# A two-layer attention and mixture-of-experts decoder: where the expert weights are kept first, and the router's stretch by quarters

## What is computed

```
h  = x + W_out( sum_b sigmoid(g_b(xn)) * (branch_b(xn) @ W_branch_b) ),  xn = RMSNorm(x)   # the mixer, three branches
xn = RMSNorm(h)
group  = top-1 of 4 (softmax of xn @ w_rg + b_rg)
expert = top-2 of the 8 in that group (xn @ w_re + b_re), weights renormalised, times the group's
out = h + sum over the chosen experts of w * ( silu(xn @ w1[e]) * (xn @ w3[e]) ) @ w2[e]     # 32 experts, 256 hidden
```

## Time and profile before

| | |
|---|---|
| three runs, median (range) | 1061.05 us (1058.94 to 1063.56) |
| the profiled execution: its own time, its span | 1065.5 us, 1063.8 us |
| TensorE matmul, weight load, VectorE, ScalarE, share of the span | 90%, 73%, 45%, 44% |
| granted TensorE clock, mean | 0.968 |
| HBM read | 291 MB, mean 275 GB/s |
| layer 0: mixer, router, experts | to 290 us, to 322 us, to 529 us |
| layer 1: mixer, router, experts | from 538 us to 815 us, to 847 us, to 1056 us |

### The profile page before, as it was taken

One profiled execution on the slowest core, in us unless ns is written; L12 is line 12 of the kernel. 1 busy time (PEld: TensorE's weight loads), 2 busy tenths in 40 slices (PEclk: granted clock), 3 DMA queues, 4 the chain that ended last, 5 costly groups with the idle time before them and its releaser, 6 DMA issues. The chain is left out here.

```text
span 1063.8 us, 19005 instructions
## 1 busy us (share of the span) xinstructions
PE 960.0 (90%) x7790; PEld 774.5 (73%) x7790; DVE 481.7 (45%) x805; ACT 472.1 (44%) x714; POOL 21.6 (2%) x39
## 2 busy tenths in 40 slices
PE   5999999999978999897669999999999789899875
PEld 5998899899865555563368988998998655565443
DVE  5446775567752213121254567655585622121112
ACT  6455555465433333322354565565654333333211
POOL 1010100000000000000000100000000000000000
PEclk9999999999989999998889999999999899999987
DMA  8644544556866999999945245535668499999994
GB/s 279 218 141 158 165 159 159 199 189 230 344 267 263 419 420 419 419 418 420 382 151 195 101 159 165 198 120 198 247 254 361 168 364 419 419 419 419 419 418 169
DMA packets 85479, 293.36 MB, mean 276 GB/s; under 512 B 16976, under 2 KB 17040, under 8 KB 60816
## 3 DMA queue, kind: packets, MB, share of 16 engines
q1 hardware_dynamic: 85392, 292.12, 71.7%
HBM read 291.05 MB, written 1.05 MB: 275 GB/s over the span
## 5 line engine op out<-in xcount | busy, mean ns | idle before, releaser
L1079 ACT ACTIVATE w_high<-weight_ring 128x1024 fp32r<-128x1024 f32 x168 | 176.8, 1060 | 212.0 <-PE ps_a L686 153.5
L1347 DVE TENSOR_TENSOR w_low<-weight_ring,w_high 128x1024 fp32r<-128x1024 f32 x168 | 202.9, 1226 | 140.7 <-ACT w_high L1079 140.1
L684 PE MATMUL ps_a<-xnT_high,w_high 128*128 128x256 f32 x704 | 203.1, 289 | 4.2 <-DVE xnT_low L1353 4.2
L686 PE MATMUL ps_a<-xnT_high,w_low 128*128 128x256 f32 x704 | 200.6, 285 | 0.0
L685 PE MATMUL ps_a<-xnT_low,w_high 128*128 128x256 f32 x704 | 200.2, 284 | 0.0
L684 PEld LDWEIGHTS ps_a<-xnT_high,w_high 128*128 128x128 f32 x704 | 134.8, 192 | 7.0 <-DVE xnT_low L1353 4.9
L685 PEld LDWEIGHTS ps_a<-xnT_low,w_high 128*128 128x128 f32 x704 | 135.1, 192 | 0.5 <-issue 0.5
L686 PEld LDWEIGHTS ps_a<-xnT_high,w_low 128*128 128x128 f32 x704 | 134.5, 191 | 0.0
L1716 DVE TENSOR_TENSOR y_lo<-ps_b,y_hi 128x512 fp32r<-128x512 f32 x64 | 44.3, 692 | 153.0 <-ACT y_hi L1318 150.4
L1049 PEld LDWEIGHTS ps_b<-fold,h 128*128 128x128 f32 x512 | 70.3, 203 | 34.4 <-issue 24.4
L1280 ACT ACTIVATE h<-ps_b 128x512 f32<-128x512 f32 x64 | 38.2, 597 | 115.3 <-PE ps_b L972 115.3
(11 more groups left out here) (326 smaller groups left out, 1508.9 us busy)
## 6 DMA issues: line engine op xcount, KB each, us to landing
weight_ring<-in_w_in_dram SPq DMA_DIRECT2D x64, 1024.0 KB, 5.3
units_over_splits<-in_w_dram SPq DMA_DIRECT2D x60, 1024.0 KB, 17.2
units_over_attention<-in_w_dram SPq DMA_DIRECT2D x48, 1024.0 KB, 16.1
weight_ring<-in_w_dram SPq DMA_DIRECT2D x40, 1024.0 KB, 15.6
units_over_branches<-in_w_dram SPq DMA_DIRECT2D x30, 1024.0 KB, 15.6
weight_ring<-in_w_branch_dram SPq DMA_DIRECT2D x12, 1024.0 KB, 5.7
unit_over_gates<-in_w_dram SPq DMA_DIRECT2D x10, 1024.0 KB, 17.2
weight_ring<-in_w_out_dram SPq DMA_DIRECT2D x8, 1024.0 KB, 6.8
```

The source lines that it names most:

```text
L684: mm(dst, wh, xh, start=row == 0 and s % 2 == 0, stop=False, skip_group_check=True)
L686: last = mm(dst, wl, xh, start=False, stop=row == rows - 1, skip_group_check=True)
L1079: A(mix_buf(whi, i), mix_raw(i), ACT.Copy).then_inc(hi_ready, 1)
L1347: v.tensor_tensor(mix_buf(wlo, i), mix_raw(i), mix_buf(whi, i).bitcast(F32), ALU.subtract).then_inc(lo_ready, 1)
```

## The change

- The places used once are three, and hold units 4, 5 and 9 (`ONCE_UNITS`); the third lies over `selectT0`. The ring holds all others in order, starting with unit 0. A reload waits for the ring's unit 18 places earlier. There are 75 reloads.
- Since unit 9 lies over `selectT0`, ScalarE copies the first `selectT` only behind the fourth `hidden` (`first_selT`). Since unit 5 lies over `XT1`, the gather step behind the second `hT` is left out and comes later.
- The last token tile of `out_proj` is done in two quarters of 256 columns, each with its own add, square, transposes, copy and logits. Token tile 0's second half of the logits moves ahead of the last part.
- The tokens are regrouped once into `x_grouped` (two buffers) by VectorE, and both halves of both tiles are worked out from it.
- The low half of the second tile moves behind `select`; the count of rounds moves up; the slot weights move down.
- The gather goes by token tile: 16 matmuls of tile 0, which wait for its `select` alone, then 16 of tile 1. ScalarE takes blocks 0 to 5 and VectorE 6 and 7.
- `idle_work(n)`: n matmuls of two constant matrices, 128 x 128 f32: 12 behind the last logits, 2 behind the counts, and 24 at the end of layer 0.
- The silu table is loaded behind the router's last exp; the exp table at the end of layer 0, behind the experts, and not in layer 1.

```diff
+ONCE_UNITS = (4, 5, 9)
-    t.once = [once_XT1[:, :], once_y[:, :]]
+    t.once = [once_y[:, :], once_XT1[:, :], once_selT[:, :]]
...
         hidden(2 * p + 1)
+        if p == 1:
+            steps.append(("first_selT", 0))
...
         hidden_T(2 * p + 1)
-        use_bank(p)
+        if p:
+            use_bank(p)
+    ring_units = [n for n in range(len(order)) if n not in ONCE_UNITS]
+    turn = {n: i for i, n in enumerate(ring_units)}
     def unit_buf(n):
-        return t.once[n] if n < ONCE else t.ring[(n - ONCE) % RING]
+        return t.once[ONCE_UNITS.index(n)] if n in ONCE_UNITS else t.ring[turn[n] % RING]
...
-                    for n in range(14, PLACES):
-                        sp.wait_ge(part_used, MIX_PARTS - SPLITS + 2 * ((n - 14) // 2 + 1))
-                        load_unit(sp, n)
+                    for i in range(12, RING):
+                        sp.wait_ge(part_used, MIX_PARTS - SPLITS + 2 * ((i - 12) // 2 + 1))
+                        if i == RING - 2:
+                            load_unit(sp, ONCE_UNITS[2])
+                        load_unit(sp, ring_units[i])
...
-                for n in range(PLACES, len(order)):
-                    sp.wait_ge(unit_used, used[n - RING])
-                    load_unit(sp, n)
+                for i in range(RING, len(ring_units)):
+                    sp.wait_ge(unit_used, used[ring_units[i - RING]])
+                    load_unit(sp, ring_units[i])
...
+            def third_quarter(q):
+                return out_part(pair[:, 1, 0:256], 1, q, slice(0, 256))
+            def last_quarter(q):
+                return out_part(psP[:, 3, 0:256], 1, q, slice(256, CHUNK))
+            def idle_work(count):
+                for _ in range(count):
+                    mm(ps_y[:, 0, 0:P], t.ident[:, :], t.ones[:, :], start=True, stop=True)
...
-            out_tile(1, 1).then_inc(part_used, 1)
-            second_half(0)
-            for q in range(2, PARTS):
-                out_tile(1, q).then_inc(part_used, 1)
-            logits_second(0)
-            second_half(1)
-            logits_second(1)
+            third_quarter(1)
+            last_quarter(1).then_inc(part_used, 1)
+            pe.wait_ge(xm_added, 2)
+            transposed(psA[:, 2, :], 0, 4, 4)
+            third_quarter(2)
+            last_quarter(2).then_inc(part_used, 1)
+            pe.wait_ge(xT_second, 1)
+            for k in range(4, NK):
+                last = router(k, 0)
+            last.then_inc(logits_done, 1)
+            third_quarter(3).then_inc(out_third, 1)
+            last_quarter(3).then_inc(part_used, 1)
+            pe.wait_ge(xm_added, 3)
+            transposed(psA[:, 3, :], 1, 4, 2)
+            pe.wait_ge(xm_added, 4)
+            transposed(psA[:, 2, :], 1, 6, 2)
+            pe.wait_ge(xT_third, 1)
+            for k in (4, 5):
+                router(k, 1)
+            pe.wait_ge(xT_last, 1)
+            for k in (6, 7):
+                last = router(k, 1)
+            last.then_inc(logits_done, 1)
+            idle_work(12)
             pe.wait_ge(picked, 1)
...
             last.then_inc(most_counted, 1)
+            idle_work(2)
...
             def first_rows():
-                pe.wait_ge(xn_hi_done, NT)
-                pe.wait_ge(xn_lo_done, NT)
-                pe.wait_ge(sel_ready, NT)
-                for k in range(NK):
-                    last = rows(first_bank(k), k)
-                    if k % 2:
-                        last.then_inc(rows_given, 1)
+                for tt in range(NT):
+                    pe.wait_ge(sel_ready, tt + 1)
+                    pe.wait_ge(xn_hi_done, tt + 1)
+                    for k in range(NK):
+                        mm(first_bank(k), t.xn_hi[tt][:, features], t.sel[:, tt, :, 0, :], ...)
+                        if k == 0:
+                            pe.wait_ge(xn_lo_done, tt + 1)
+                        last = mm(first_bank(k), t.xn_lo[tt][:, features], t.sel[:, tt, :, 0, :], ...)
+                        if tt == NT - 1 and k % 2:
+                            last.then_inc(rows_given, 1)
...
+            if not last_layer:
+                idle_work(24)
...
             A(t.er[:, :, :], t.er[:, :, :], ACT.Exp).then_inc(er_done, 1)
+            nc.scalar.preload_act_table_set(SILU)
...
-                for k in (0, 1, 4, 5):
+                for k in range(6):
                     act.wait_ge(rows_given, k // 2 + 1)
...
-                        if p == PAIRS - 1:
-                            nc.scalar.preload_act_table_set(EXP_LN)
...
             if not last_layer:
+                nc.scalar.preload_act_table_set(EXP_LN)
...
-            dve.wait_ge(xn_hi_done, 2)
-            v.scalar_tensor_tensor(out=t.xn_lo[1][:, :], in0=t.xg[:, :], scalar=t.rs[:, 1:2],
-                                   in1=t.xn_hi[1][:, :].bitcast(F32), op0=ALU.mult,
-                                   op1=ALU.subtract).then_inc(xn_lo_done, 1)
             dve.wait_ge(picked, 1)
...
             select(0, 0)
+            low(1)
```

More of the change, by code:

```diff
@@ L163, in tensors @@
     t.rounds = sb("rounds", [1, 1], I32)
+    whole.part(-whole.at % 64)
     t.ring_a = sb("weight_ring", [P, MIX_RING, UNIT])
@@ L245, in tensors @@
     t.XT = [sb("XT0", [P, NK, BATCH * SLOTS]), XT1]
+    sel_at = r.at
     t.sel, t.selw = sb("select", [P, NT, BATCH, 2, SLOTS], F32R), sb("select_weighted", [P, NT, BATCH, SLOTS])
-    t.xg = r.again().sb("x_grouped", [P, D])
+    t.xg = [Region(nc, at, three.end).sb(f"x_grouped_{n}", [P, D]) for n, at in (("first", sel_at), ("second", r.at))]
     t.cw = [sb(f"slot_weight{i}", [P, BATCH * SLOTS]) for i in range(2)]
@@ L444, in layer @@
     ps_h, ps_x, ps_y = t.ps_b[:, 0, :], t.ps_b[:, 1, :], t.ps_b[:, 2:4, :]
-    logits = [psP[:, 2, 64 * tt:64 * tt + NR] for tt in range(NT)]
+    logits = [psA[:, tt, 0:NR] for tt in range(NT)]
     counts = psP[:, 3, :]
@@ L1575, in _, with low @@
-            copy_xT(1)
-            sum_squares(1, sq_done, 4, msum_ready)
-            dve.wait_ge(logits_done, 2)
-            dve.wait_ge(rs_ready, 2)
-            for tt in range(NT):
-                n = ch.mark(v.scalar_tensor_tensor(out=t.lg[:, tt, :], in0=logits[tt], scalar=t.rs[:, tt:tt + 1],
-                                                   in1=t.br[:, :], op0=ALU.mult, op1=ALU.add))
-            ch.until(n)
+            def low(tt):
+                dve.wait_ge(xn_hi_done, tt + 1)
+                v.scalar_tensor_tensor(out=t.xn_lo[tt][:, :], in0=t.xg[tt][:, :], scalar=t.rs[:, tt:tt + 1],
+                                       in1=t.xn_hi[tt][:, :].bitcast(F32), op0=ALU.mult,
+                                       op1=ALU.subtract).then_inc(xn_lo_done, 1)
@@ new lines, in logits_out @@
+            def logits_out(tt):
+                dve.wait_ge(logits_done, tt + 1)
+                dve.wait_ge(rs_ready, tt + 1)
+                return ch.mark(v.scalar_tensor_tensor(out=t.lg[:, tt, :], in0=logits[tt], scalar=t.rs[:, tt:tt + 1],
+                                                      in1=t.br[:, :], op0=ALU.mult, op1=ALU.add))
+            third, last = slice(CHUNK, CHUNK + 256), slice(CHUNK + 256, D)
+            group_x(0, slice(0, CHUNK), 1)
+            dve.wait_ge(out_first, 1)
@@ new lines, in _ @@
+            add_out(0, out[1][:, 0, :], slice(CHUNK, D))
+            group_x(0, slice(CHUNK, D), 2)
+            sum_squares(0, sq_done, 3, msum_ready)
+            low(0)
+            dve.wait_ge(x_tr, 3)
+            v.tensor_copy(t.xT[:, 4:, 0:P], psA[:, 2, :].rearrange("p (k n) -> p k n", k=4)).then_inc(xT_second, 1)
+            dve.wait_ge(out_third, 1)
+            add_out(1, out[1][:, 1, 0:256], third)
+            group_x(1, third, 3)
+            dve.wait_ge(part_used, MIX_PARTS)
+            add_out(1, psP[:, 3, 0:256], last)
@@ L1585, in _ @@
+            group_x(1, last, 4)
+            logits_out(0)
+            dve.wait_ge(x_tr, 5)
+            v.tensor_copy(t.xT[:, 6:, P:], psA[:, 2, 0:256].rearrange("p (k n) -> p k n", k=2)).then_inc(xT_last, 1)
+            dve.wait_ge(sq_done, 5)
+            v.scalar_tensor_tensor(out=t.msum[:, 1:2], in0=t.sq[:, 1, 0:1], scalar=t.sq[:, 1, 1:2], in1=t.sq[:, 1, 2:3],
+                                   op0=ALU.add, op1=ALU.add).then_inc(msum_ready, 1)
+            ch.until(logits_out(1))
             four = "p t (g e) -> p t g e"
```

168 lines of the change are left out of this document (82 added, 86 removed).

## The result

The changed kernel takes **1052.25 us** at the median of 4 runs (1049.57 to 1053.49); beside it the kernel before took 1062.3 (4 runs). The ratio is 0.9915, 95% interval 0.9886 to 0.9944. Timed again in a later series it took 1051.22 us beside 1062.52: 0.9897 (0.9877 to 0.9917). By the two ratios it is 9 to 11 us faster. The forecast was 1048.6 us, 12.4 us less than before, with a range of 1042.5 to 1055.5.

The account below looks back on a forecast made before the run. Reloads standing in line at the DMA engines were taken to bound the expert stages. Gains of 2 x 6.6 us less 0.8 at the end of layer 0 gave 12.4, so 1061.05 - 12.4 = 1048.6 us, range 1042.5 to 1055.5.

Parts of the forecast that it names:

- Quarters: End of `out_proj` and logits, done by quarters: taken as 0, at most 1 us gained or 1 us lost.
- Gather start and constants: Router: gather starts 1.05 us earlier, at full clock with the constant matmuls; `hidden` begins 3.55 us earlier.
- The rival of half clock in the gather: Gap still too long for the clock: `hidden` gains 1.3 us, not 3.55; 1053.1 us; chance 0.18.
- Left-out step: First steps of the experts: leaving out the gather step behind the second `hT` gains 1.3 us.
- Late `selectT` copies: First steps of the experts: the first scatter waits for copies behind the fourth `hidden`; 1.4 us lost.
- Sum at unit 10: TensorE 3.45 us ahead after the experts' first steps (3.55 + 1.3 - 1.4); unit 10 frees its place at 867.8, not 871.22.
- Order of the units: Expert stage: eighth reload waits for unit 10; last landing at 1041.1, not 1047.7, a gain of 6.6 us per layer.
- 67 x 2.51: Expert stage: the 67 reloads that land after the eighth follow at 2.51 us each.
- Tail: Last landing to the end: taken as now; at most 2.9 us less, or 3.2 us more at half clock.
- the rival with both tails at full clock: Both layers' ends keep full clock: 2 x 2.9 us less, 1042.8 us; chance 0.05.
- End of layer 0: 24 constants 0.4 us late, exp table delays the squares 0.3, five more semaphores 0.1: 0.8 us lost.
- Constants at half clock: Router gap: constants take 0.43 us each and block TensorE's queue; +7.7 us, 1068.7 us; chance 0.05.

Follow-up runs that it names:

- 1: Changed kernel with its three once-places holding units 0, 1 and 9, so the first reload waits for unit 2 again; 1053.78 us, ratio 0.9919.
- 2: Changed kernel without the third once-place, and with the `selectT` copies back behind the first `hidden`; 1050.16 us, ratio 0.9892.
- 3: Changed kernel without the third once-place, the `selectT` copies staying behind the fourth `hidden`; 1054.69 us, ratio 0.9926.
- 5: Kernel before with units 4 and 5 in its two once-places and the gather step behind the second `hT` left out; 1054.50 us, ratio 0.9933.
- Experiment 7: Kernel before with units 4 and 5 once-placed, the step behind the second `hT` left out, and 12 and 2 gap constants; 1053.00 us, ratio 0.9913.
- experiment 4: Changed kernel without the 12 and the 2 constant matmuls in the router's gap; 1056.68 us, ratio 0.9957.
- 8: Changed kernel without the 24 constant matmuls at the end of layer 0; 1048.33 us, ratio 0.9865.
- 6: Kernel before with only the 12 constant matmuls behind the last logits and 2 behind the counts added; 1061.86 us, ratio 0.9998.

## Why the prediction was right

**What bounds.** Right. The line of reloads sets each layer's end, and the reload that waits for unit 10 sets the line within 1 to 2 us (experiments 1, 2, 3, 5). A full line and a gap ahead of unit 10 are both in the trace: the DMA engines stand idle for 2.5 us ahead of the first reload and for some 2 us ahead of unit 10's (forecast: twice 2 to 4).

**Quarters.** Taken as 0: the last pick ends 21.6 us behind the zero before and 21.3 after. Experiment 7, without them, is as fast as the changed kernel within what the times can tell, but it lacks other parts of the change too, so the quarters are not tested by themselves.

**Gather start and constants.** Forecast 1.05 earlier at full clock, measured 1.44 with the granted clock at 1.00. `hidden`: forecast 3.55 earlier, measured 3.87 (3.49 in layer 0), set by ScalarE's six copies. The rival of half clock in the gather did not come true here; experiment 4 shows what it would have cost, and that its price of 2.25 us was too high, since the clock came back after 12 matmuls.

**First steps of the experts.** Left-out step: forecast 1.3, measured 1.4 (from `hidden` to unit 10's reload, 24.5 us before and 23.1 in experiment 5). Late `selectT` copies: forecast 1.4, measured 1.35 (24.89 us against 23.53 in experiment 2). One term was missing: the slot weights wait 0.34 us for `select_weighted`, which the change moved down. Sum at unit 10: forecast 3.45 earlier, measured 3.48 (3.12 in layer 0). That it fits so well is luck: 0.3 more at `hidden` stands against the wait that was missing.

**Order of the units.** The mechanism was right; the failing term is **67 x 2.51**. I took the pace from the GB/s of 870 to 1045 us, where the line of the kernel before is full, and for that line it holds: the 67 units behind unit 10's reload took 2.515 us each there from landing to landing (2.527 in layer 0). In the changed kernel a unit takes 2.534 us in layer 1 and 2.548 in layer 0, because behind unit 10's landing four units in layer 1 and five in layer 0 take 2.9 to 4.0 us in place of 2.49. So 2.51 is 1.6 and 2.5 us too little for 67 units. The rows had a hint: from the first landing to the last it is (1047.7 - 857.7) / 75 = 2.533 us a unit, and one unit soon after the start of the line took 4.2. A line that runs dry and starts again seems to pay for one slow unit more. In the changed kernel, its repetition, 4 and 8, one of the first five units behind unit 10's landing takes 3.6 to 4.0 us in both layers; in the kernel before, whose line is full by then, none of the first twenty takes over 2.9. The cause of the slow units is open. With 4.7 in place of 5.1 for the first wait the last landing comes 5.4 us earlier in layer 1 and 4.2 in layer 0, not 6.6 in each: 3.6 us of the gain that was forecast. 12.4 less 3.6 is 8.8, beside the 9.4 that the traces leave for the change and the 9 to 11 of the two series.

**Tail.** Taken as now within bounds of 3 us down and up. From the last landing to the end of the last `y_hi` copy it is between 2.7 and 6.0 us in the 14 profiles, in either layer, depending on where the clock falls ahead of it: 5.1 to 6.0 in the nine stages in which a stretch of 10.2 us at 0.50 ends within 2.1 us ahead of the last landing, and 2.7 to 4.4 in the other nineteen. In the changed kernel's profile layer 0 had such a stretch (5.4 us, 1.1 more than before) and layer 1 had not (2.9 us, 2.7 less than before; 1.5 less to the end of the span). So it was neither "as now" nor the rival with both tails at full clock. In the second profile of the changed kernel both tails were short (2.7 and 3.0), and that execution took 1050.35 us and not the rival's 1042.8. The tail is a draw in each execution.

**End of layer 0.** The constants hold the barrier up by 0.4 to 0.5: right. The exp table was to cost 0.3 and costs nothing: the first square starts 1.55 us behind the last `y_hi` copy, 1.54 before, and waits for VectorE, not for ScalarE. The load ends at 522.30 and the square starts at 522.55. The Trainium skill (ScalarE: Activation LUTs, What ACT_TABLE_LOAD costs) has 1.38 us of drain on top of the load for a change of table. By that (an estimate) the square would start no earlier than 523.7. It starts at 522.55, so here too, as in the earlier trace rows, the trace does not agree.

**Constants at half clock**, the rival on the other side: the twelve take 2.92 us (forecast 2.64 at full clock, 5.2 at half), and TensorE waits 1.01 us for the picks behind them. It never came near.

## What to carry to other kernels

Where transfers stand in line and the line runs dry once, look for the last transfer that is issued when the line is empty or nearly so: here its issue time and the number behind it set the end within 1 to 2 us, and what was spent ahead of it (a third place, a head start of 5 us) brought little or nothing. Take the pace of the line from landing to landing over the whole stage, and look at how it starts again after it ran dry. And when filler work keeps the clock in one gap, read the next 20 us too: here the next pair of short waits took it in its place, and the filler paid only once a small step was moved out from between them.

## What the runs showed of the hardware

The first 30 us of the program, the same instructions in every kernel, do not always take the same time. ScalarE's first copy of `ps_a` behind the first projection in three kernels' timelines (8, changed, 6):

```profile
29.05 1.01 ACT L1167 ACTIVATE sb_qT<-ps_a 128x1024 f32<-128x1024 f32 x1
```

```profile
30.35 1.01 ACT L1169 ACTIVATE sb_qT<-ps_a 128x1024 f32<-128x1024 f32 x1
```

```profile
31.70 1.01 ACT L1128 ACTIVATE sb_qT<-ps_a 128x1024 f32<-128x1024 f32 x1
```

The 2.7 us are there at the first `out_tile` too, with 1.6 us more where the clock fell once, to 0.50 from 206 to 210 (before, and kernels 1 and 6). Together with the two tails, up to 3 us each, this is of the size of the spread between executions of one kernel (the kernel before: 1055.3 to 1065.5 us), and a profile has to be read from a zero inside it.

The clock did not fall in long idle time only, as in the 3.76 us of experiment 4. It also fell behind waits of 0.80 and 0.64 us with matmuls between them (6), after 2.29 us of work in 3.40, and in one layer of 7 within a wait of 1.41 us, but not in the other. The prediction took full clock for a stretch because more than half of it would be work; that came true for the gather, and in 6 the same ground would have misled.
